# K pages turned on VectorE in 32x32 blocks, and scores in sixteen TensorE tiles

## The chip, the cores and the metric

The kernel runs on one core of a Trainium2 chip. The metric is device time in microseconds (us), from the start of the program to its end. A TensorE "pass" below is one matmul record of the profile with its weight load: a matmul on f32 operands leaves two such records, one on fp32r operands leaves one.

## The reference

One step of a small hybrid decoder: a gated short-convolution layer, then shared keys and values, then one attention layer with per-head forget values. The part that the change touches is the attention of the 64 new sample tokens (8 sequences of 8 tokens, 16 heads of 64) over 2048 past keys a sequence, which lie in 16 pages of 128 rows:

```python
s = jnp.einsum('nqhd,nkhd->nhqk', q, k).astype(jnp.float32) * (HEAD_DIM ** -0.5)
s = s + (jnp.transpose(fq, (0, 2, 1))[:, :, :, None] - jnp.transpose(fk, (0, 2, 1))[:, :, None, :])
p = jax.nn.softmax(jnp.where(mask[None, None], s, -jnp.inf), axis=-1)
return jnp.einsum('nhqk,nkhd->nqhd', p.astype(v.dtype), v)
```

`page_table` says which pages of `cache_k` and `cache_v` belong to a sequence. A page of K or of V is 128 rows of 1024 floats, 512 KB.

## The kernel before

After the convolution layer (to about 300 us) and the projection of all queries (to about 364 us), a loop of eight rounds does the rest; it is called `heads(i)` on every engine. Round i does two things at once: the past attention of sample sequence i over its 16 K pages and 16 V pages, and for the pair of heads 2i, 2i+1 the projection of K, V and the gate z, and the prompt's attention in four blocks. A last stage (from about 899 us) merges the new tokens and multiplies by the output weights.

**Pages.** SyncE loads them (`load_page`, L374 to L377) into a ring of 8 slots, 8 pages ahead, in the order K0 to K15, V0 to V15. A K page's slot is free when TensorE has turned it (wait on `b_t1`, L432), a V page's when its product is done (`b_used`, L434). In the same queue, in order, stand the round's other loads: `f_broad` at n=0, one weight block of 512 KB at n=0, 4 and 12, one `suffix` block of 256 KB at n=4, 8, 12 and 16, each behind waits of its own.

**Scores of a K page.** TensorE turns the page with 8 transposes of 128x128 (`turn`, L1201) into two PSUM banks; ScalarE copies one half out (L666) and VectorE the other (L1009). Two pages make a unit. `unit_scores` (L1393) multiplies the turned unit by the queries in 8 matmuls, each 128 rows by 32 columns of the array (four column tiles), 256 columns of data, f32. VectorE adds the forget term and takes the maximum (`add_suffix`, L1014). There are 8 units a round. Between the pages TensorE does single pieces of the K and V projections (`project` and `piece`, L1221; a piece is six matmuls; 8 pieces make one projection).

**After the last unit** TensorE turns the new K and V rows, and does the first prompt block's scores. VectorE makes the shift of the softmax, ScalarE takes exp of the scores (L707, four parts), and TensorE turns the four parts into `p_turned`. Then the 16 V pages follow (L1519), with the prompt's blocks between them. The sum of squares for the norm of the new K (L1426, L1427) stands among the K pages (k == 9), and ScalarE, then GpSimd (L514), finish that norm there.

**The end of a round.** VectorE multiplies the prompt's output by the gate (L1123), ScalarE copies it as fp32r (L766), and VectorE takes the difference (L1127).

All engines run their own instruction order as written; nothing but semaphores ties them.

Of the kernel before, what the change touches and what calls it, by code (L numbers as in the profile page):

```python
# [31 lines left out]
P = 128  # L32
# [20 lines left out]
STREAM = 2 * NPG  # L53
SLAB = 256
# [46 lines left out]
def build(nc, ctx, x_prompt, x_sample, state_conv, cache_k, cache_v, cache_logf, page_table,  # L101
# [33 lines left out]
    KTS = [place("k_turned", [P, KT, 2 * PAGE])]  # L135
    PTS = place("p_turned", [P, NPG, P])
    KTS.append(place("k_turned_odd", [P, KT, 2 * PAGE], over=at["p_turned"]))
# [36 lines left out]
    QC = place("q_current", [P, KT, 32])  # L174
# [7 lines left out]
    CS = place("logf_sums", [P, H, PAGE], over=at["sample_scores"])  # L182
    STN = place("state_rows", [2 * NB, D], over=at["suffix"])
# [5 lines left out]
    WHB = place("w_high_b", [P, KT, SLAB], F32R, over=at["k_turned"])  # L189
# [8 lines left out]
    QF = place("queries", [P, KT, TOK], over=at["gated_high"])  # L198
    FA = place("f_raw", [H, TOK], over=at["k_t"])
# [46 lines left out]
    b_used, b_qc, b_qt = sem("v_page_used"), sem("q_current_ready"), sem("q_pair_ready")  # L246
# [49 lines left out]
    def _(sp):  # L296
# [77 lines left out]
        def load_page(b, n):  # L374
            page = sp.value_load(PTAB[0:1, bass.ds(b * NPG + n % NPG, 1)], min_val=0, max_val=n_pool - 1)
            src = (kpages if n < NPG else vpages)[bass.ds(page, 1), :, :]
            sp.dma_start(ring[:, n % RING, :], src.rearrange("a p n -> (a p) n")).then_inc(b_page[n % RING], 16)  # L377
# [23 lines left out]
        def heads(i, last):  # L401
            for n in range(STREAM):
                if n == 0:
                    sp.wait_ge(b_c0f, 8 * i)
                    sp.wait_ge(b_c1f, 8 * i)
# [10 lines left out]
                if n in (4, 8, 12, 16):  # L416
                    c = n // 4 + 1
                    if not (last and c >= 4):
                        sp.wait_ge(b_c1f, 8 * i + n // 4)
                        load_suffix(i + c // 4, c % 4)  # L420
# [21 lines left out]
        sp.wait_ge(b_t1f, 24 * NB)  # L442
# [17 lines left out]
    def _(pool):  # L460
# [29 lines left out]
        for b in range(NB):  # L490
            pool.dma_start(suffix_dram[b].rearrange("h (g n) -> g h n", g=NPG),
                           CS[b * NPG:(b + 1) * NPG, :, :]).then_inc(s_sfx_st, 16)
# [10 lines left out]
        for n in range(10):  # L503
            scale_b(n % 2, n // 2 + 1, G_B if n < KT else G_KV)
        pool.wait_ge(q_out, KT)
        pool.tensor_copy(QC[:, :, :], QZ[:, 0, :, :]).then_inc(b_qc, 1)
        pool.tensor_copy(QT[:, :], QF[:, 0, 0:SEQ]).then_inc(b_qt, 1)

        def heads(i, last):
# [5 lines left out]
            if not last:  # L515
                scale_b(1, 7 + 2 * i, G_KV)
                pool.wait_ge(b_c1, 8 * i + 4)
                pool.tensor_copy(QC[:, :, :].rearrange("p k n -> p (k n)"),
                                 QZ[:, bass.ds(i + 1, 1), :, :].rearrange("p a k n -> p (a k n)")).then_inc(b_qc, 1)
                pool.wait_ge(b_c0, 8 * i + 8)  # L520
                pool.wait_ge(b_c1, 8 * i + 8)
# [8 lines left out]
    def _(act):  # L530
# [124 lines left out]

        act_done = ch.n


        def heads(i, last):
            t0 = [0]  # L660

            def turned0(out, src):

                act.wait_ge(b_t0, 24 * i + t0[0] + 1)
# [3 lines left out]
            for k in range(NPG):  # L668
                c = (k % 2) * PAGE
                if k % 2 == 0 and k >= 4:  # L670
                    act.wait_ge((b_c0, b_c1)[k // 2 % 2], 8 * i + k // 4)
                turned0(KTS[k // 2 % 2][:, 0:4, c:c + PAGE],
                        PS[:, T0, :].rearrange("p (k n) -> p k n", k=4)).then_inc(b_t0f, 1)
                if k == 6:
                    pr, sa = both(D0)
                    act.wait_ge(b_proj, KT + 3 * i + 1)
                    act.wait_ge(b_gl, i)
                    act.wait_ge(b_ddve, i + 1)
                    act.activation(prompt2(SQ[:, 0:SEQ]), pr, ACT.Square)
                    act.activation(SQ[:, SEQ:TOK], sa, ACT.Square).then_inc(b_dact, 1)  # L680
                if k == 10:
                    high_b(KT + 3 * i + 2, 1)
                if k == 14:
                    pr, sa = both(D0)
                    act.wait_ge(b_proj, KT + 3 * i + 2)
                    act.activation(prompt2(VT[:, 0:SEQ]), pr, ACT.Copy)
                    act.activation(VT[:, SEQ:TOK], sa, ACT.Copy).then_inc(b_dact, 1)
                if k == 9:

                    act.wait_ge(b_ss, i + 1)  # L690
                    act.wait_ge(b_normed, i)
                    act.activation(RR[:, SEQ:TOK], PS[:, OS, 0:NS], ACT.Ln, bias=EPSB(P), scale=1.0 / HD)
                    act.activation(RR[:, 0:SEQ], PS[:, OP, :], ACT.Ln, bias=EPSB(P), scale=1.0 / HD).then_inc(b_ln, 1)
                    act.wait_ge(b_ln, i + 1)
                    act.activation(RR[:, :], RR[:, :], ACT.Exp, scale=-0.5).then_inc(b_rr, 1)
            if not last:
                high_b(KT + 3 * i + 3, 0)

            act.wait_ge(b_kpo, 16 * i)
            act.wait_ge(b_vpo, 16 * i)  # L700
            turned0(KN[:, 0:QB, :], PS[:, T0, :].rearrange("p (k n) -> p k n", k=4)).then_inc(b_t0f, 1)
            turned0(VN[:, :, :], PS[:, T0, :].rearrange("p (k n) -> p k n", k=4)).then_inc(b_t0f, 1)
# [10 lines left out]
            act.wait_ge(b_t0f, 24 * i + 18)  # L713
            act.wait_ge(b_t1f, 24 * i + 17)
# [45 lines left out]
            assert t0[0] == 24  # L760
# [32 lines left out]
    def _(dve):  # L793
# [129 lines left out]
        def low_b(n, slot, to=None):  # L923
# [5 lines left out]
        dve.tensor_tensor(CS[:, :, :], PS[:, 7, 0:H].unsqueeze(2).to_broadcast([P, H, PAGE]), CS[:, :, :],  # L929
                          ALU.subtract).then_inc(s_sfx, 1)  # L930
# [38 lines left out]
        def query(m, s):  # L969
# [3 lines left out]
            dve.scalar_tensor_tensor(prompt2(QF[:, bass.ds(m, 1), 0:SEQ].rearrange("p a n -> p (a n)")), pr, GQ[:, 0:1],  # L973
                                     prompt2(RR[:, 0:SEQ]), ALU.mult, ALU.mult)
# [26 lines left out]
        def heads(i, last):  # L1001
# [3 lines left out]
            def turned1(out, src):  # L1005

                dve.wait_ge(b_t1, 24 * i + t1[0] + 1)
# [3 lines left out]
            def add_suffix(u):  # L1011

                free, bank = ((b_c0f, C0), (b_c1f, C1))[u % 2]
                dve.tensor_tensor_reduce(  # L1014
                    SS[:, u * 256:(u + 1) * 256], PS[:, bank, 0:256],
                    SFX[:, (u // 2) % 2, (u % 2) * 256:(u % 2) * 256 + 256],
                    1.0, NEG, ALU.add, ALU.max, TINY[:, 4 + u:5 + u]).then_inc(free, 1)

            for k in range(NPG):
                c = (k % 2) * PAGE  # L1020
                if k % 2 and k >= 3:
                    u = k // 2 - 1
                    if u % 2 == 0:
                        dve.wait_ge(b_sfx[(u // 2) % 2], (2 * i + u // 4 + 1) * 16)
# [613 lines left out]
```

## Time and profile before

| | us |
|---|---|
| median of 3 runs (lowest, highest) | 971.62 (970.4, 973.45) |
| the profiled execution | 975.04 |
| its span, first to last instruction | 973.2 |

In a row of a timeline the first number is the start in us from the start of the span, the second the duration in us, then come the engine, the line of the kernel, the operation, what it writes and reads, and how many instructions were merged. In brackets stands how long the engine had been idle before, and who ended that.

### The profile page before, as it was taken

The numbers are of one execution on the slowest core, as the hardware profiler recorded it, in microseconds if no ns is written. First come the engines' busy times: TensorE is split into PE (matmuls) and PEld (weight loads), VectorE is DVE, ScalarE is ACT, GpSimd is POOL, SyncE is SP. The second block draws the span as 40 slices with busy tenths as digits, with TensorE's granted clock in tenths as the row PEclk, the third lists the DMA queues.
The fourth block names the chain that finished last, engine by engine and source line by source line (L and its number), as shares of the span: only waits on it lengthen the run. The fifth ranks groups of instructions, "written<-read, shape, count | busy, mean of one in ns | idle before, by whom it ended". The sixth has DMA issues, their size and how long they took to land.

```text
span 973.2 us, 23705 instructions
## 1 busy us (share of the span) xinstructions
PE 939.5 (97%) x8516; PEld 802.0 (82%) x8516; DVE 486.6 (50%) x1133; ACT 385.1 (40%) x728; POOL 167.4 (17%) x111
## 2 busy tenths in 40 slices
PE   4999999999999999999999999999999999999998
PEld 4999999999998987868768778688687686776898
DVE  5675444556355334554544544645545545445632
ACT  5333333332144443543444534535434445345210
POOL 2233444332030311102002002011020020000000
PEclk9999999999999999999999999999999999999999
DMA  7233222225343527799799798798996997987412
GB/s 233 66 87 86 86 76 75 85 65 130 120 165 103 174 55 228 254 329 341 237 360 313 249 364 290 247 376 261 315 350 237 362 323 244 365 297 249 142 44 98
DMA packets 133334, 206.41 MB, mean 212 GB/s; under 512 B 8848, under 2 KB 91457, under 8 KB 133171
## 3 DMA queue, kind: packets, MB, share of 16 engines
q1 hardware_dynamic: 121602, 198.35, 60.7%
q10 hardware_dynamic: 11168, 5.51, 2.0%
q0 software_dynamic: 528, 2.10, 0.8%
q8 instruction: 21, 0.34, 0.2%
q14 instruction: 15, 0.11, 0.0%
HBM read 195.29 MB, written 10.63 MB: 212 GB/s over the span
## 4 chain that ended last, share of the span: by engine, by line
PE 82%; DMA 7%; ACT 4%; DVE 4%; issue 2%; SPq 1%; ACTq 0%; DVEq 0%
PE psum L1221 40%; PE psum L1201 16%; PE psum L1270 9%; PE psum L1404 7%; PE psum L1519 4%; DMA page_ring<-in_cache_k 4%; ACT sample_scores L707 2%; DMA w_raw<-in_a_w_out 2%; PE psum L1469 1%; PE psum L1447 1%; DMA residual<-in_x_prompt 1%; PE psum L1319 1%; PE psum L1427 1%; PE psum L1449 1%; DMA page_ring<-in_cache_v 1%
## 5 line engine op out<-in xcount | busy, mean ns | idle before, releaser
L1221 PE MATMUL psum<-xn_high,w_high 128*128 128x256 f32 (+1 forms) x992 | 237.2, 318 | 2.6 <-DVE w_low L832 2.6
L1221 PE MATMUL psum<-xn_low,w_high 128*128 128x256 f32 (+1 forms) x992 | 216.4, 297 | 0.0
L1221 PE MATMUL psum<-xn_high,w_low 128*128 128x256 f32 (+1 forms) x992 | 216.3, 297 | 0.0
L1221 PEld LDWEIGHTS psum<-xn_high,w_high 128*128 128x128 f32 x992 | 163.9, 191 | 20.2 <-issue 16.6
L1221 PEld LDWEIGHTS psum<-xn_high,w_low 128*128 128x128 f32 x992 | 169.0, 191 | 0.0
L1221 PEld LDWEIGHTS psum<-xn_low,w_high 128*128 128x128 f32 x992 | 168.9, 190 | 0.0
L1201 PE MATMUL psum<-constants,page_ring 128*128 128x128 f32 x1024 | 137.5, 277 | 7.7 <-DMA page_ring<-in_cache_k 6.5
L1201 PEld LDWEIGHTS psum<-constants,page_ring 128*128 128x128 f32 x1024 | 114.8, 141 | 35.1 <-issue 33.4
L501 POOL TENSOR_TENSOR w_raw<-w_raw,gains 128x1024 f32<-128x1024 f32 x32 | 60.8, 1899 | 338.9 <-DMA w_raw<-in_b_w_in 220.7
L1009 DVE COPY k_turned_odd<-psum 128x512 f32<-128x512 f32 x64 | 44.2, 691 | 93.5 <-PE psum L1201 93.5
L832 DVE TENSOR_TENSOR w_low<-w_raw,w_high 128x1024 fp32r<-128x1024 f32 x32 | 51.4, 1606 | 72.6 <-ACT w_high L565 72.6
L1009 DVE COPY k_turned<-psum 128x512 f32<-128x512 f32 x64 | 44.2, 690 | 71.5 <-PE psum L1201 71.3
L478 POOL TENSOR_TENSOR w_raw<-w_raw,gains 128x1024 f32<-128x1024 f32 x30 | 62.5, 2083 | 88.7 <-DMA w_raw<-in_a_w_in 88.7
L666 ACT ACTIVATE k_turned<-psum 128x512 f32<-128x512 f32 x64 | 38.2, 597 | 96.5 <-PE psum L1201 96.4
L1519 PE MATMUL psum<-page_ring,p_turned 128*32 128x256 f32 x1024 | 75.2, 388 | 0.9 <-DMA page_ring<-in_cache_v 0.8
L565 ACT ACTIVATE w_high<-w_raw 128x1024 fp32r<-128x1024 f32 x32 | 33.9, 1060 | 89.0 <-PE psum L1221 63.5
L666 ACT ACTIVATE k_turned_odd<-psum 128x512 f32<-128x512 f32 x64 | 38.1, 596 | 71.3 <-PE psum L1201 71.3
L1270 PE MATMUL psum<-w_high,gated_high 128*128 128x256 f32 (+1 forms) x160 | 46.5, 290 | 4.4 <-DVE w_low L859 1.9
L926 DVE TENSOR_TENSOR w_low<-w_raw,w_high 128x1024 fp32r<-128x1024 f32 x30 | 36.9, 1231 | 18.2 <-ACT w_high L615 18.2
L1270 PE MATMUL psum<-w_low,gated_high 128*128 128x256 f32 (+1 forms) x160 | 45.7, 286 | 0.0
L1270 PE MATMUL psum<-w_high,gated_low 128*128 128x256 f32 (+1 forms) x160 | 45.7, 286 | 0.0
L1270 PE MATMUL psum<-w_high_b,gated_high 128*128 128x256 f32 (+1 forms) x160 | 45.3, 283 | 0.1
(236 smaller groups left out, 1420.2 us busy)
## 6 DMA issues: line engine op xcount, KB each, us to landing
page_ring<-in_cache_k SPq DMA_DIRECT2D x128, 512.0 KB, 5.6
page_ring<-in_cache_v SPq DMA_DIRECT2D x128, 512.0 KB, 4.8
w_raw<-in_a_w_in SPq DMA_DIRECT2D x30, 512.0 KB, 4.1
suffix<-suffix_scratch SPq DMA_DIRECT2D x32, 256.0 KB, 4.8
w_raw<-in_b_w_in SPq DMA_DIRECT2D x16, 512.0 KB, 6.2
w_raw<-in_kv_w SPq DMA_DIRECT2D x16, 512.0 KB, 6.1
w_raw<-in_a_w_out SPq DMA_DIRECT2D x4, 1024.0 KB, 5.1
f_broad<-f_scratch SPq DMA_DIRECT2D x8, 512.0 KB, 6.2
```

The source lines that it names most:

```text
L478: pool.tensor_tensor(WR[:, q % 2, :, :], WR[:, q % 2, :, :], gain(G_A), ALU.mult).then_inc(a_scaled, 1)
L501: pool.tensor_tensor(WR[:, slot, :, :], WR[:, slot, :, :], gain(g), ALU.mult).then_inc(b_scaled, 1)
L565: act.activation(WH[:, slot, :, :], WR[:, slot, :, :], ACT.Copy).then_inc(a_high, 1)
L666: return act.activation(out, src, ACT.Copy)
L832: dve.tensor_tensor(WL[:, slot, :, :], WR[:, slot, :, :], WH[:, slot, :, :].bitcast(F32), ALU.subtract).then_inc(a_split, 1)
L926: dve.tensor_tensor(lo, WR[:, slot, :, :], h.bitcast(F32), ALU.subtract).then_inc(b_split, 1)
L1009: return dve.tensor_copy(out, src)
L1201: return pe.transpose(out, src, CT[0:r, C_ID:C_ID + r])
L1221: mm = pe.matmul(PS[:, bank + h, 0:c.stop - c.start], w[:, k, :], x[:, k, c], start=(k == 0 and n == 0), stop=(k == KT - 1 and n == 2))
L1270: mm = pe.matmul(PS[0:r, bank, 0:SLAB], x[:, k, toks(t)], wp[:, k, :], start=(k == 0 and p == 0), stop=(k == KT - 1 and p == 2))
L1404: mm = pe.matmul(PS[32 * j:32 * j + 32, bank, 0:256], QC[:, 2 * j + pp, :], KTS[u % 2][:, 2 * j + pp, :], start=(pp == 0), stop=(pp == 1), ...
L1519: mm = pe.matmul(PS[32 * j:32 * j + 32, OS, 0:4 * HD], PTS[:, k, 32 * j:32 * j + 32], ring[:, n % RING, 4 * HD * j:4 * HD * (j + 1)], star ...
```

## The change

1. VectorE turns each K page where it lies in the ring, with one `transpose` of 128x1024 that turns each block of 32x32 by itself. The transposes by TensorE and the copies of `k_turned` by ScalarE and VectorE are gone.
2. Four pages make a unit, so there are 4 units a round. `unit_scores` has 128 matmuls on 32 rows by 32 columns of the array (16 tiles), 128 columns of data each, f32; row tile r writes the bank C0+r, so the four banks C0, C1, OP, OS hold a unit's scores, and one matmul of a single column on bfloat16 stands ahead of them.
3. The queries lie in blocks for that (`q_blocks`), made once a round by GpSimd from `q_quarters`, which 16 matmuls make once, ahead of the loop.
4. TensorE's first part of a round is a loop of two, in each four pieces, a unit, four pieces, a unit; the pieces are the K projection's in the first and the V projection's in the second. The squares and the whole of the gate projection follow.
5. The ring's K slots come free four at a time, when a unit is scored. V pages are read in another order of rows, since the scores come out with their rows in that order; the `suffix` values are stored so too.
6. VectorE's order in a round: turns of pages 4 to 7, `add_suffix(0)`, copies of the K projection, turns 8 to 10, `add_suffix(1)`, turns 11 to 13, the low half of the gate's weights, turns 14 and 15, `add_suffix(2)` and `(3)`. Turns 0 and 1 of the next round stand ahead of the output's gating, 2 and 3 behind it.

```diff
@@ SyncE
                     if n < NPG:
-                        sp.wait_ge(b_t1, 24 * i + n + 1)
+                        if n % GROUP == 0:
+                            sp.wait_ge(b_su, NG * i + n // GROUP + 1)
                     else:
                         sp.wait_ge(b_used, NPG * i + n - NPG + 1)
@@ ScalarE, the order in a round
+            act.activation(prompt2(SQ[:, 0:SEQ]), pr, ACT.Square)
...
+            high_b(KT + 3 * i + 2, 1)
...
+            act.activation(prompt2(VT[:, 0:SEQ]), pr, ACT.Copy)
...
+            act.wait_ge(b_ss, i + 1)
...
+            act.activation(RR[:, 0:SEQ], PS[:, T1, :], ACT.Ln, bias=EPSB(P), scale=1.0 / HD).then_inc(b_ln, 1)
...
+            act.activation(RR[:, :], RR[:, :], ACT.Exp, scale=-0.5).then_inc(b_rr, 1)
...
+            turned0(VN[:, :, :], PS[:, T0, :].rearrange("p (k n) -> p k n", k=4)).then_inc(b_t0f, 1)
+            turned0(KN[:, 0:QB, :], PS[:, T0, :].rearrange("p (k n) -> p k n", k=4)).then_inc(b_t0f, 1)
             if not last:
                 high_b(KT + 3 * i + 3, 0)
...
             act.wait_ge(b_nbs, i + 1)
@@ VectorE
+        def turn_pages(i, ks):
+            for k in ks:
+                dve.wait_ge(b_page[k % RING], (4 * i + k // RING + 1) * 16)
+                dve.transpose(ring[:, k % RING, :], ring[:, k % RING, :]).then_inc(b_kt, 1)
@@
+            if not last:
+                turn_pages(i + 1, range(2))
             dve.wait_ge(b_po, i + 1)
             dve.wait_ge(b_sz, i + 1)
             dve.tensor_tensor(SQ[:, 0:SEQ], PS[:, OP, :], SZ[:, 0:SEQ], ALU.mult).then_inc(b_gf, 1)
...
             dve.tensor_tensor(gl, SQ[:, 0:SEQ], gh.bitcast(F32), ALU.subtract).then_inc(b_gl, 1)
+            if not last:
+                turn_pages(i + 1, range(2, GROUP))
@@ TensorE
+            def unit_scores(a, u):
+                pe.wait_ge(b_kt, NPG * i + 2 * GROUP * a + GROUP * (u + 1))
+                pe.wait_ge(b_suf, NG * i + 2 * a + u)
+                pe.matmul(PS[:, OS, 511:512], IDB[:, :], CMB[:, 0:1], start=True, stop=True)
+                for xf in range(8):
                     for j in range(4):
+                        c = 8 * j + xf
+                        for r in range(4):
+                            mm = pe.matmul(PS[32 * j:32 * j + 32, C0 + r, 0:P], QD[32 * r:32 * r + 32, c, :],
+                                           ring[32 * r:32 * r + 32, GROUP * u:GROUP * (u + 1), 32 * c:32 * c + 32],
+                                           start=(xf == 0), stop=(xf == 7), tile_position=(32 * r, 32 * j))
+                mm.then_inc(b_su, 1)
...
+            with pe.Fori(0, 2) as a:
+                pieces(a, range(0, 4))
+                pe.wait_ge(b_qd, i + 1)
...
+                pe.wait_ge(b_gf, i)
+                unit_scores(a, 0)
+                pieces(a, range(4, 8))
+                unit_scores(a, 1)
```

## Rows read from the trace of the kernel before

**Rows 1.** The page: TensorE's busy time, and GB/s of all DMA in 40 slices.
```profile
PE 939.5 (97%) x8516; PEld 802.0 (82%) x8516; DVE 486.6 (50%) x1133; ACT 385.1 (40%) x728; POOL 167.4 (17%) x111
GB/s 233 66 87 86 86 76 75 85 65 130 120 165 103 174 55 228 254 329 341 237 360 313 249 364 290 247 376 261 315 350 237 362 323 244 365 297 249 142 44 98
```
**Rows 2.** The chain of waits of the whole run, and one piece of it.
```profile
PE 82%; DMA 7%; ACT 4%; DVE 4%; issue 2%; SPq 1%; ACTq 0%; DVEq 0%
...
628.20 5.28 DMA page_ring<-in_cache_k
```
**Rows 3.** Engines by stretch: K pages of a round, then the rest of it.
```profile
633.60:670.50 36.90, 36.84 (x346) 30.90 (x347) 15.74 (x35) 14.61 (x26) 6.82 (x4) 1.00 1.01 347
671.50:700.30 28.80, 27.61 (x297) 18.19 (x293) 17.43 (x61) 15.64 (x40) 1.01 (x2) 1.00 0.79 258
```
**Rows 4.** TensorE's timeline among the K pages of a round.
```profile
638.59 1.03 PE L1201 MATMUL psum<-constants,page_ring 128*128 128x128 f32 x8
639.38 0.51 PE L1221 MATMUL psum<-xn_high,w_high 128*128 128x256 f32 x2
...
640.35 1.07 PE L1404 MATMUL psum<-k_turned,q_current 128*32 128x256 f32 x16
641.35 1.09 PE L1201 MATMUL psum<-constants,page_ring 128*128 128x128 f32 x8
```
**Rows 5.** Groups by line and shape, TensorE: all transposes of K pages.
```profile
L1201 PE MATMUL psum<-constants,page_ring 128*128 128x128 f32 x1024 | 137.5, 277 | 7.7 <-DMA page_ring<-in_cache_k 6.5 <-DVE k_turned L1009 1.2
```
**Rows 6.** TensorE's timeline: two row tiles side by side, and four column tiles.
```profile
608.18 0.92 PE L1447 MATMUL psum<-k_t,q_t 64*128 64x384 f32 x4
...
898.97 1.99 PE L1537 MATMUL psum<-ks_t,q_spread 128*32 128x64 f32 x128 [0.17 <-issue]
```
**Rows 7.** One line of VectorE: count, shortest, median and longest duration in ns.
```profile
L926 DVE TENSOR_TENSOR w_low<-w_raw,w_high x30: 1206/1219/1624, 311.4 to 861.2; 128x1024 fp32r<-128x1024 f32 x30
```
**Rows 8.** SyncE's timeline of DMA issues over the start of a round.
```profile
628.20 9.01 SPq L377 DMA_DIRECT2D page_ring<-in_cache_k  x8
637.92 0.40 SPq L407 DMA_DIRECT2D f_broad<-f_scratch  x1
...
639.94 4.16 SPq L377 DMA_DIRECT2D page_ring<-in_cache_k  x4
...
649.73 4.13 SPq L377 DMA_DIRECT2D page_ring<-in_cache_k  x4
```
**Rows 9.** DMA issues of 630 to 641, then of 633.6 to 646: count, KB, median us to landing.
```profile
page_ring<-in_cache_k SPq DMA_DIRECT2D x7, 512.0 KB, 5.8
...
page_ring<-in_cache_k SPq DMA_DIRECT2D x7, 512.0 KB, 7.3
```
**Rows 10.** Timelines of TensorE, VectorE and ScalarE where one round ends and the next begins.
```profile
633.60 1.09 PE L1201 MATMUL psum<-constants,page_ring 128*128 128x128 f32 x8 [0.70 <-DMA page_ring<-in_cache_k]
...
632.92 0.69 DVE L1123 TENSOR_TENSOR squares<-psum,silu_z 128x512 f32<-128x512 f32 x1
634.53 0.69 DVE L1127 TENSOR_TENSOR gated_low<-squares,gated_high 128x512 f32 x1 [0.93 <-ACT gated_high L766]
...
633.74 0.63 ACT L766 ACTIVATE gated_high<-squares 128x512 f32 x1 [0.29 <-DVE squares L1123]
```
**Rows 11.** Timelines behind the last unit of a round: ScalarE, TensorE, and GpSimd's norm.
```profile
608.68 0.71 ACT L707 ACTIVATE sample_scores<-sample_scores,tiny 128x512 f32<-128x512 f32 x1
...
604.30 1.07 PE L1404 MATMUL psum<-k_turned_odd,q_current 128*32 128x256 f32 x16
...
614.23 0.64 PE L1519 MATMUL psum<-page_ring,p_turned 128*32 128x256 f32 x8
...
657.93 1.43 POOL L514 TENSOR_TENSOR k_t<-k_t,rsqrt 128x576 f32<-128x576 f32 x1 [2.51 <-ACT rsqrt L695]
```
**Rows 12.** TensorE after an idle time, and the granted clock of the stretch that follows.
```profile
902.85 0.36 PE L1270 MATMUL psum<-w_high,gated_high 128*128 128x256 f32 x1 [1.88 <-DVE w_low L859]
...
904.00:908.00 4.00, 4.00 (x25) 4.00 (x24) 1.55 (x7) 2.41 (x15) 0.00 (x0) 0.62 0.88 287
```

More of the change, by code:

```diff
@@ L53 @@
 STREAM = 2 * NPG
+GROUP = 4
+NG = NPG // GROUP
 SLAB = 256
@@ L504, in _, with block_queries @@
             scale_b(n % 2, n // 2 + 1, G_B if n < KT else G_KV)
+        def block_queries(b):
+            own = QN[:, bass.ds(b, 1), 0:2 * H * NQ].rearrange("p a (j x f q) -> p x (a j) f q", x=4, f=2, q=NQ)
+            to = QD[:, :, :].rearrange("p (j x f) n -> p x j f n", x=4, f=2)
+            for x in range(4):
+                ins = pool.tensor_copy(to[:, x, :, :, NQ * x:NQ * x + NQ], own[:, x])
+            ins.then_inc(b_qd, 1)
+        pool.wait_ge(b_proj, 2)
+        pool.memset(QD[:, :, :], 0.0).then_inc(s_qz, 1)
         pool.wait_ge(q_out, KT)
-        pool.tensor_copy(QC[:, :, :], QZ[:, 0, :, :]).then_inc(b_qc, 1)
         pool.tensor_copy(QT[:, :], QF[:, 0, 0:SEQ]).then_inc(b_qt, 1)
+        pool.wait_ge(s_qne, 4)
+        pool.wait_ge(s_qz, 1)
+        block_queries(0)
         def heads(i, last):
@@ L662, in turned0 @@
             def turned0(out, src):
-                act.wait_ge(b_t0, 24 * i + t0[0] + 1)
+                act.wait_ge(b_t0, 8 * i + t0[0] + 1)
                 t0[0] += 1
                 return act.activation(out, src, ACT.Copy)
[L668 to L695, printed above, removed]
@@ new lines, in heads @@
+            turn_pages(i, range(4, 8))
+            add_suffix(0)
+            dve.wait_ge(b_proj, KT + 3 * i + 1)
+            pr, sa = both(D0)
+            gk = GAIN[:, G_K:G_K + 1]
+            dve.tensor_scalar(prompt2(KN_T[:, 0:SEQ]), pr, gk, None, ALU.mult)
+            dve.tensor_scalar(KN_T[:, SEQ:TOK], sa, gk, None, ALU.mult).then_inc(b_ddve, 1)
+            turn_pages(i, range(8, 11))
+            add_suffix(1)
+            turn_pages(i, range(11, 14))
+            low_b(KT + 3 * i + 2, 1)
@@ L1362, in _ @@
         pe.wait_ge(s_fnr, 1)
+        pe.wait_ge(q_out, KT)
+        pe.wait_ge(s_bf, 3)
+        for c in range(4):
+            for r in range(4):
+                mm = pe.matmul(PS[32 * r:32 * r + 32, T0 + c, :].rearrange("p (m n) -> p m n", m=KT),
+                               CT[:, C_ID + 32 * c:C_ID + 32 * c + 32], QF[:, :, SEQ:TOK],
+                               start=True, stop=True, tile_position=(0, 32 * r))
+        mm.then_inc(s_qn, 1)
         def heads(i):
@@ L1388, in project @@
                 for k in ks:
[L1389 removed]
+                    mm = piece(1, k, D0)
                 if ks[-1] == KT - 1:
                     mm.then_inc(b_proj, 1)
[L1393 to L1407 removed]
@@ new lines, in pieces @@
+            def pieces(a, ks):
+                with pe.If(a):
+                    if ks[0] == 0:
+                        pe.wait_ge(b_t0f, 8 * i)
+                        pe.wait_ge(b_t1f, 8 * i)
+                    for k in ks:
+                        mm = piece(0, k, T0)
+                    if ks[-1] == KT - 1:
+                        mm.then_inc(b_proj, 1)
+                with pe.Else():
+                    if ks[0] == 0:
+                        pe.wait_ge(b_split, KT + 3 * i + 2)
+                        pe.wait_ge(b_sz, i)
+                    for k in ks:
+                        mm = piece(1, k, D0)
+                    if ks[-1] == KT - 1:
+                        mm.then_inc(b_proj, 1)
@@ L1437, in block_scores @@
+            pe.matmul(PS[:, T1, :], CT[:, C_ONESB:C_ONESB + P], SQ[:, 0:SEQ], start=True, stop=True).then_inc(b_ss, 1)
             def block_scores(r):
```

246 lines of the change are left out of this document (110 added, 136 removed).

## The prediction, as it was made before the result was known

> **What bounds the kernel now.** I read the page first. TensorE is busy 97% of the span, twice as much as any other engine [rows 1], and 82% of the chain of waits is its work [rows 2]. That says: take work off TensorE. The second view speaks against it. In the eight rounds all DMA moves 240 to 376 GB/s, up from 66 to 90 in the first stage [rows 1], and by stretch the DMA engines are busy for 1.01 of the time among the K pages of a round, at 347 GB/s, and for 0.79 in the rest [rows 3]. The one DMA piece that recurs in the chain is K page 0 of the next round [rows 2]; TensorE waits 0.70 us for it [rows 10]. So TensorE sets the time, and right behind it stands the supply of pages. A round takes 700.3 - 633.6 = 66.7 us; I count its time from 633.0, where TensorE ended the round before, 0.7 ahead of 633.60.
>
> **When the pages come (kept by the change).** SyncE issues 8 K pages from 628.20 in 9.01 us [rows 8], one in (9.01 - 0.34) / 7 = 1.24 us. Page 0 lands 5.28 us after its issue [rows 2], at +0.5 us of the round; the others follow 1.24 to 1.28 apart, so page 3 at about +4.5 and page 7, issued at 636.9 and landing after 5.8 [rows 9], at +9.7. Behind them stand `f_broad` and a weight block. Pages 8 to 11 are issued from 639.94 over 4.16 us, the last at 643.8, and land after 7.3 us [rows 8, 9]: page 11 at +18.1. Pages 12 to 15 are issued to 653.5 and, by the 5.8 to 7.3 us of rows 9, land to about +27. In all that time the queue is full [rows 3], so an earlier issue brings none of them earlier.
>
> **Part 1, turning on VectorE.** TensorE loses 128 transposes a round: 8 in 0.79 us (638.59 to 639.38) [rows 4], 16 times: 12.6 us bare, and 137.5 / 8 = 17.2 us by the group [rows 5]. VectorE gets 16 turns of 128x1024 f32. No row shows one. From below: 1024 elements can't take less than the 0.69 us of a 512-element line [rows 10], in a faster mode, 0.7 us. From above: twice the two-input line on as many elements, 2.4 us. The nearest row is that line itself, 1.22 us [rows 7]; I take 1.25. It takes 20 us of VectorE, which sheds 16 copies of 0.69.
> The Trainium skill, "Vector Engine (DVE) Microarchitecture Reference", The reshape front-end and per-opcode configuration, says that a 32x32 transpose is pipelined to one element a cycle and lane. No row shows it; by it the turn would cost as the row on 1024 elements, and the sum stays.
>
> **Part 2, the scores.** Gone: 8 units of 16 passes, 1.00 us each (640.35 to 641.35) [rows 4]: 8.0 us a round. New: 4 units of 128 matmuls, 256 passes each. A pass of 256 columns on four column tiles costs 1.00 / 16 = 62 ns, with the switch of shape in it. One of 64 columns costs 1.77 us / 128 = 14 ns: its 128 passes are 1.99 us long [rows 6], less the last one's 0.22. Per column and tile that is 14 x 4 / 64 = 0.87 ns. Row tiles too run side by side: 4 passes of 384 columns on two row tiles take 0.92 us [rows 6], where one after the other they would be 4 x 384 x 0.87 = 1.34. 128 columns are then 111 ns a pass, by 16 tiles 7 ns: 256 x 7 = 1.8 us a unit at best. At 14 ns, the densest issue that a row shows, it is 3.6 us. At worst 16 tiles run as four: 111 / 4 = 28 ns, 7.1 us. I take 9 ns, between the first two, and 0.3 for the switch: 2.6 us.
> The trace has passes at 14 ns. The Trainium skill, "TensorE: Matmul & The Clock Gate", Wait — 56ns, not 53.3ns?, says that start-to-start never drops below about 25 ns; the trace disagrees for tiles. By that rule a unit would be 6.4 us, an estimate, and the whole the rival of slow tiles below.
>
> **Part 3, the round's start.** VectorE turns page 0 at +0.5 to 1.8, page 1 to 3.1. The gating (0.69), ScalarE's copy and VectorE's difference stand behind that now: 632.92 to 635.22 is 2.3 us [rows 10], so they end at 5.3. Pages 2 and 3 are turned by 7.8. TensorE has four pieces ahead of the first unit, 4 x 0.8 = 3.2 us (639.38 to 640.35 is one, 0.97 with the switch) [rows 4], and then waits 4.5 us. Unit 0: 7.8 to 10.4. Four pieces to 13.6. Pages 4 to 7 are turned by 12.8; unit 1: 13.6 to 16.2. Slots 0 to 3 come free at 10.4, so pages 8 to 11 are issued 11.2 to 14.9, 3 to 4 us later than before, and still land to +18.1 or little later. `add_suffix(1)` (512 elements, 0.7 us by rows 10) and page 11 end at 20; unit 2: 20 to 22.6, pieces to 25.8. Pages 12 to 15 are issued behind unit 1 and land to +27; page 15 is turned at 28.9 behind the weights' low half, 1.22 [rows 7]. Unit 3: 29.0 to 31.6. Before, the last unit ended 18.8 + 8.9 us ahead of the round's end [rows 11], at +39.0. So 7.4 us come in here, of the 12.6 + 8.0 - 4 x 2.6 = 10.2 that TensorE is given.
>
> **Part 4, behind the last unit.** Before, exp began 608.68 - 605.37 = 3.3 us after it, and the first V page 8.9 us after it (614.23) [rows 11]. Now the squares (1.1 us) stand there, then ScalarE's two Ln and Exp (1.7 us by the 0.7 of rows 11), and GpSimd's 1.43 us [rows 11] to +4.4; TensorE's three gate pieces (2.4), V turns and a fourth piece cover that to +4.9. Then come the K turns (0.5), ScalarE's copy (0.6) and its high half of weights, moved behind that copy (some 1.1 us for twice the elements of its copy). Exp begins at +7.3, 4.0 later than before, and the rest follows as before: first V page at +12.9. The V pages keep their 633.0 - 614.23 = 18.8 us.
> A round: 31.6 + 12.9 + 18.8 = 63.3 us against 66.7: 3.4 less, eight times 27 us.
>
> **Part 5, once.** 16 matmuls of 512 columns ahead of the loop are 32 passes on four column tiles, twice the columns of a 62 ns pass: 4.0 us. The copies behind them stand beside the first four pieces. The sum: -27 + 4 = -23 us. Against its own 975.04 us that is 952; against the median, 3.4 us lower, 949. I predict 950.
>
> **Costs set at nothing.** The copies taken from ScalarE were hidden: it is busy 40% [rows 1]. GpSimd's `block_queries` waits for the last unit of a round and has 30 us until the next first one. The V pages' new order of rows keeps 4 KB a row; a costlier issue would delay V0 to V7, which have about 5 us to spare. SyncE waits for a unit with `suffix` and weight blocks queued behind; their users come later than before.
>
> **The rivals.**
> *Dear turns (slower).* A turn of 2.1 us makes VectorE the chain of the first part: from +0.5, 16 turns and 6.5 us of its other lines put unit 3 at +40.6 instead of 29.0, the round at 74.9, the whole at 952 + 8 x 11.6 = 1045. It decides from 1.6 us on, where the round is 66.7. For it: nothing shows the instruction. Against: 1.22 us for as many elements with two inputs.
> *Slow tiles (slower).* With 7.1 us a unit TensorE's own order binds: 7.8 + 4 x 7.1 + 9.6 = 45.8, the round 77.5, the whole 952 + 8 x 14.2 = 1066. It decides from 4.4 us a unit. For it: the two passes of a matmul go to one tile, and the second must wait for the first. Against: four tiles keep this pace already.
> *The change of bound costs the gain (within 15 us of before).* TensorE now idles 4.5 us at each start. After 1.88 us idle the granted clock was 0.62 over 904 to 908, that is 1.2 GHz for three of those 4 us [rows 12]. One such fall a round where TensorE binds costs half of the three, 1.5 us, and a page later by one service time 1.3: 65 to 66.5 a round, 962 to 977. For it: both are in the rows.
> *TensorE alone sets the time (faster).* Then a round loses 12.6 + 8.0 and gains 4 x 2.6: 56.5 us, 897 in all. Against: 1.01 DMA share among the K pages [rows 3]. Half of it, should pages come earlier than I have them: 925 to 937.
>
> **How the numbers follow.** My forecast, 938 to 962: 0.50. TensorE alone or half of it: 0.12. The gain lost: 0.17. Dear turns 0.09, slow tiles 0.12. The likeliest gives 950. The range of 922 to 1000 takes in the first, the third, half of the second and the slow rivals' mild forms (a turn of 1.75 us, a unit of 5 us give about 1000): 0.79. A measurement tells 0.3% from no change, 2.9 us: faster 0.71 (the first two and half of the third), same 0.05, slower 0.24.
>
> **What would show it.** Turns near 1.25 us on VectorE; units of 2 to 3.6 us on TensorE; an idle time of 4 to 5 us ahead of each round's first unit, ended by a VectorE turn, and one ahead of the fourth; DMA share near 1 in the first 27 us of a round; first V page 12 to 13 us after the last unit; rounds of 63 us. Units over 4.4 us, turns over 1.6 us or rounds under 60 us make it wrong.

## The result: 1047.03 us, 7.9% slower, and its profile

The changed kernel takes 1047.03 us (1045.41 to 1050.35, 4 runs) against 971.01 (970.16 to 973.45, 4 runs): ratio 1.0787, interval 1.0757 to 1.0817. The forecast was 950 us. Ratios compare the fast executions of each kernel; where only one execution is fast, the table calls the ratio unclear. From the profile's page of the changed kernel (busy time; queue of instruction packets: packets, MB, share; costliest groups):

```profile
PE 915.1 (87%) x14724; PEld 795.0 (76%) x14724; DVE 570.3 (54%) x1111; ACT 311.3 (30%) x602; POOL 176.2 (17%) x136
...
q8 instruction: 86, 1.41, 0.5%
...
PE 65%; issue 11%; DMA 11%; DVE 4%; SPq 4%; ACT 4%; ACTq 0%; DVEq 0%
...
L1014 DVE STREAM_TRANSPOSE page_ring<-page_ring 128x1024 f32<-128x1024 f32 x128 | 154.0, 1229 | 51.1 <-DMA page_ring<-in_cache_k 50.5
...
L1433 PE MATMUL psum<-page_ring,q_blocks 32*32 32x128 f32 x8192 | 124.5, 291 | 26.8 <-issue 26.8
```

TensorE was relieved, from 97% to 87% [rows 1], and the time rose all the same. What took the room is named in the chain, where "issue" has 11% after 2% before [rows 2]: time in which TensorE waited for nothing that the profile shows. Its waits (total, times, longest, in us):

```profile
PE psum L1251 <- issue: 46.8, 15, 6.8
PE psum L1433 <- issue: 26.8, 16, 2.4
PE psum L1428 <- DVE tiny L1052: 13.3, 8, 3.0
```

73.6 us of TensorE's idle time have no releaser. One round in TensorE's timeline (start, duration, idle time before in brackets), from the last V page of a round to the last unit of the next and its end:

```profile
671.20 0.64 PE L1551 MATMUL psum<-page_ring,p_turned 128*32 128x256 f32 x8 [0.68 <-DMA page_ring<-in_cache_v]
678.63 0.82 PE L1251 MATMUL psum<-xn_high,w_high 128*128 128x256 f32 x2 [6.80 <-issue]
...
684.69 2.69 PE L1433 MATMUL psum<-page_ring,q_blocks 32*32 32x128 f32 x187
688.66 1.16 PE L1433 MATMUL psum<-page_ring,q_blocks 32*32 32x128 f32 x69 [1.28 <-issue]
...
693.17 1.99 PE L1433 MATMUL psum<-page_ring,q_blocks 32*32 32x128 f32 x136
697.24 2.22 PE L1433 MATMUL psum<-page_ring,q_blocks 32*32 32x128 f32 x120 [2.07 <-issue]
...
703.96 3.57 PE L1433 MATMUL psum<-page_ring,q_blocks 32*32 32x128 f32 x256
...
711.91 3.57 PE L1433 MATMUL psum<-page_ring,q_blocks 32*32 32x128 f32 x256
...
728.01 0.64 PE L1551 MATMUL psum<-page_ring,p_turned 128*32 128x256 f32 x8
...
747.02 0.64 PE L1551 MATMUL psum<-page_ring,p_turned 128*32 128x256 f32 x8 [0.25 <-DMA page_ring<-in_cache_v]
```

A round runs from 671.84 to 747.66: 75.8 us, against 66.7 before [rows 3] and 63.3 forecast. TensorE stands still for 6.80 us at its start though the profile shows nothing that the pieces there wait for, and stops in the middle of units 0 and 1. Units 2 and 3, the inner loop's second pass, run through. Unit 0 starts at +12.9. Unit 3 ends at +43.6, forecast 31.6; the first V page follows 12.5 us behind it and the V pages take 19.7. So all of the loss lies ahead of unit 3's end. The windows of the same round (the last three columns are granted clock, DMA share, GB/s):

```profile
671.90:682.00 10.10, 3.37 (x14) 3.40 (x15) 8.49 (x9) 1.01 (x2) 0.00 (x0) 0.63 1.03 404
682.00:695.00 13.00, 11.72 (x430) 10.60 (x428) 4.96 (x8) 0.76 (x3) 1.90 (x1) 0.90 0.35 108
```

Over the idle start and the pieces behind it the granted clock is 0.63 on average, that is 1.2 GHz for about three quarters of these 10.1 us. Unit 0 frees its slots late, and the DMA engines, which were full ahead of it, fall to 0.35.

### The profile page after: what moved, and what is told of

It is laid out like the page before. It is cut to its first block, busy times and chain, and to the rows that moved or that the text cites. A ratio compares the mean times of both kernels' runs of the same rounds, so it can differ in the third digit from the quotient of the medians.

```text
span 1048.5 us, 35591 instructions
## 1 busy us (share of the span) xinstructions
PE 915.1 (87%) x14724; PEld 795.0 (76%) x14724; DVE 570.3 (54%) x1111; ACT 311.3 (30%) x602; POOL 176.2 (17%) x136
## 4 chain that ended last, share of the span: by engine, by line
PE 65%; issue 11%; DMA 11%; DVE 4%; SPq 4%; ACT 4%; ACTq 0%; DVEq 0%
PE psum L1251 36%; PE psum L1433 9%; PE psum L1300 9%; DMA page_ring<-in_cache_v 5%; PE psum L1231 3%; PE psum L1551 3%; DMA suffix<-suffix_scratch 2%; SPq L379 2%; DMA page_ring<-in_cache_k 2%; ACT sample_scores L724 2%; SPq L384 2%; DMA w_raw<-in_a_w_out 1%; PE psum L1482 1%; PE psum L1504 1%; DMA residual<-in_x_prompt 1%
## 5 line engine op out<-in xcount | busy, mean ns | idle before, releaser
L1251 PEld LDWEIGHTS psum<-xn_high,w_high 128*128 128x128 f32 x992 | 175.7, 201 | 74.2 <-issue 70.2
L1251 PE MATMUL psum<-xn_low,w_high 128*128 128x256 f32 (+1 forms) x992 | 224.5, 307 | 0.0
L1014 DVE STREAM_TRANSPOSE page_ring<-page_ring 128x1024 f32<-128x1024 f32 x128 | 154.0, 1229 | 51.1 <-DMA page_ring<-in_cache_k 50.5
L1251 PEld LDWEIGHTS psum<-xn_low,w_high 128*128 128x128 f32 x992 | 178.0, 200 | 0.0
L1251 PEld LDWEIGHTS psum<-xn_high,w_low 128*128 128x128 f32 x992 | 176.8, 199 | 0.0
L1433 PE MATMUL psum<-page_ring,q_blocks 32*32 32x128 f32 x8192 | 124.5, 291 | 26.8 <-issue 26.8
L1433 PEld LDWEIGHTS psum<-page_ring,q_blocks 32*32 32x32 f32 x8192 | 103.9, 105 | 37.7 <-issue 31.1
L1052 DVE CUSTOM_DVE_ANT_1 sample_scores<-psum,suffix 128x512 f32<-128x512 f32 x32 | 34.4, 1076 | 29.5 <-issue 29.5
L938 DVE TENSOR_TENSOR residual<-psum,residual 128x256 f32<-128x256 f32 (+1 forms) x40 | 16.6, 420 | 55.1 <-PE psum L1300 54.9
L1551 PEld LDWEIGHTS psum<-page_ring,p_turned 128*32 128x32 f32 x1024 | 23.0, 108 | 29.5 <-issue 13.4
```

The lines of the kernel that those rows point to most:

```text
L1014: dve.transpose(ring[:, k % RING, :], ring[:, k % RING, :]).then_inc(b_kt, 1)
L1052: dve.tensor_tensor_reduce(out, PS[:, C0:OS + 1, 0:P], later, 1.0, NEG, ALU.add, ALU.max, TINY[:, 4 + u:5 + u]).then_inc(b_suf, 1)
L1251: mm = pe.matmul(PS[:, bank + h, 0:c.stop - c.start], w[:, k, :], x[:, k, c], start=(k == 0 and n == 0), stop=(k == KT - 1 and n == 2))
L1433: mm = pe.matmul(PS[32 * j:32 * j + 32, C0 + r, 0:P], QD[32 * r:32 * r + 32, c, :], ring[32 * r:32 * r + 32, GROUP * u:GROUP * (u + 1), 32 ...
L1551: mm = pe.matmul(PS[32 * j:32 * j + 32, OS, 0:4 * HD], PTS[:, k, 32 * j:32 * j + 32], ring[:, n % RING, 4 * HD * j:4 * HD * (j + 1)], star ...
```

## The experiments

Two theories are put to the test, S and U. Theory S: the 6.80 us are TensorE waiting for its instructions. The page has 86 instruction packets, the kernel before 21; the rounds' body grew from 1,390 to 1,877 instructions (counted in the compiled program), and in the 450 us from 450 to 900 the trace of the kernel before has none of that queue. Theory U: the time lies in the work (units, suffix additions, the gating).

The trace also says when each of these packets is under way (0.9 to 1.5 us each in after's rounds), and that ties them to the stops. In the round shown, one packet runs from 675.46 to 676.43, and TensorE goes on at 678.63; one from 686.22 to 687.18, and it goes on at 688.66; one from 694.82 to 695.87, and it goes on at 697.24. In the rounds of after there are 23 stops put down to issue that are longer than 0.8 us. All of them end behind the end of a packet, by 1.3 to 1.5 us inside the units and by 2.2 to 2.4 us at a round's start. In a_flat it is 1.2 to 1.6 us for all 28 such stops, in b_pad_flat 1.3 to 1.8 us for all 20. Chance would not do that: in after the packets come 8 us apart on average.

| kernel | what differs | us | ratio to before (95%) |
|---|---|---|---|
| b_two | before, body of two rounds | 1001.65 | 1.0344 (1.0295 to 1.0393) |
| b_flat | before, rounds written out | 976.05 | 1.0059 (1.0038 to 1.0080) |
| b_pad_loop | before, 256 more passes a round, looped | 1019.08 | 1.0488 (1.0459 to 1.0518) |
| b_pad_flat | the same, written out | 1098.91 | 1.1328 (1.1268 to 1.1388) |
| a_flat | after, all loops written out | 1128.92 | 1.1661 (1.1616 to 1.1705) |
| a_inner | after, inner loop written out | 1136.58 | 1.1729 (1.1696 to 1.1761) |
| a_outer | after, outer loop written out | 1064.50 | 1.0953 (1.0892 to 1.1013) |
| a_onepath | after, If and Else merged | 1046.92 (1017.55 to 1057.12) | unclear |
| a_wide | after, units of half the instructions | 996.25 | 1.0300 (1.0240 to 1.0360) |
| a_wide84 | a_wide, wider matmuls | 1003.10 | 1.0326 (1.0286 to 1.0365) |
| a_wide_light | a_wide, half of the K bytes | 960.53 | 0.9896 (0.9852 to 0.9940) |
| a_wide_turns | a_wide, two turns earlier | 978.29 | 1.0064 (1.0039 to 1.0089) |
| b_coarse | before, K slots reloaded by fours | 973.04 | 1.0036 (1.0015 to 1.0057) |
| a_light | after, half of the K bytes | 1007.65 | 1.0369 (1.0316 to 1.0422) |

**Does the length of the program alone cost time? b_two, b_flat, b_pad_loop, b_pad_flat.** No part of the change is in these four.

```
 b_two:   for i2 in Fori(0, NB // 2):  heads(2 * i2); heads(2 * i2 + 1)
 b_flat:  for i in range(NB):  heads(i)
 b_pad_loop, ahead of unit 7:
+    with pe.Fori(0, 8) as q:
+        for n in range(4):          # b_pad_flat: for n in range(32), no Fori
+            for j in range(4):
+                pe.matmul(PS[32*j:32*j+32, OS, 508:509], CT[:, 32*j:32*j+32], CT[:, 0:1], ...)
```

> The kernel before with one edit: TensorE's loop runs four times over two rounds instead of eight times over one, so its body is some 2,780 instructions instead of 1,390; the work and every wait are the same. Theory S: the body no longer fits, each of the four jumps costs 5 to 8 us, 20 to 35 us more than before (990 to 1010 us), and the trace has instruction packets in the rounds, where before has none. Theory U: within 3 us of before.

> The kernel before with TensorE's eight rounds written out straight, no jump at all. Theory S in its narrow form (only the jump back costs, straight code is fetched ahead in time): within 5 us of before, with some 45 instruction blocks fetched over the rounds. Theory S in its wide form (any fetch costs, whichever way it is reached): 15 us or more slower. Theory U: within 3 us of before.

> The kernel before with 128 more matmuls a round on TensorE (32x32 tiles, one column, into a PSUM column that nobody reads), 512 instructions, written as a loop of 8 times 64 instructions: the rounds' body has 1,459 instructions. At the 14 ns a pass of before's tiles they take 3.6 us a round, 29 us in all. Theory S (instruction supply, store somewhere between 1,390 and 1,880 instructions): the body still fits, some 1,000 us, no instruction packets in the rounds. Theory U: some 1,000 us.

> The same 128 matmuls a round in the same place, written out: the body has 1,902 instructions, as many as after's 1,877, and TensorE executes the same matmuls as in the looped twin. Theory S: the body is fetched anew in each round, 30 to 60 us above the twin (1,030 to 1,060 us), with 7 to 9 instruction blocks a round in the trace and an idle time of 5 to 7 us put down to issue at each round's start. Theory U: the twin's time within 3 us.

The instruction packets on the pages of b_two, b_flat, b_pad_loop and b_pad_flat, one line each:

```profile
q8 instruction: 66, 1.08, 0.4%
```
```profile
q8 instruction: 58, 0.95, 0.4%
```
```profile
q8 instruction: 21, 0.34, 0.1%
```
```profile
q8 instruction: 93, 1.52, 0.6%
```

b_two does the work of before and takes 32 us more, as theory S expected. The padded pair executes the same matmuls and differs by 79.8 us: its bodies have 1,459 and 1,902 instructions, and only the longer one brings packets into the rounds. TensorE's longest stops in b_pad_flat, in the added matmuls and at the round's start behind them:

```profile
655.98 1.63 PE L1476 MATMUL psum<-constants 128*32 128x1 f32 x174
660.83 1.33 PE L1476 MATMUL psum<-constants 128*32 128x1 f32 x82 [3.22 <-issue]
...
698.80 1.96 PE L1201 MATMUL psum<-constants,page_ring 128*128 128x128 f32 x8 [5.66 <-issue]
```

That is the picture of the changed kernel in one that has nothing of the change. Theory U is refuted for these; theory S's sizes were too low (the pair was expected 30 to 60 us apart, and the looped one at 1,000 us; of the looped one's 48 us its added passes take 8 x 4.00 = 32, the rest was not taken apart). b_flat shows the other side: written out, each round's 1,390 instructions are fetched too (58 packets), but TensorE has no stop of any weight put down to issue, and it costs 6 us in all. That this is so because they are used up slowly, 1,390 in 66.7 us, fits, but no run varies it alone.

**Is it the jump or the rate? a_flat, a_inner, a_outer, a_onepath.**

```
 a_inner:  for a in range(2): ... if a: ... else: ...   (in place of pe.Fori, pe.If, pe.Else)
 a_flat:   a_inner, and for i in range(NB): heads(i)
 a_outer:  after, and for i in range(NB): heads(i)
 a_onepath, pieces(a, ks): no If; PS[:, bass.ds(2 * a + h, 1), ...], WH[:, 0, k, :] in both passes
```

> The kernel after with TensorE's program written out straight: its eight rounds one behind the other and the two halves of the K part as Python code, so that no branch is taken in the rounds; waits, matmuls and the other engines are the same. Theory S (instruction supply: the rounds' loop body of TensorE no longer stays in its instruction store and each jump back costs TensorE some 6.8 us idle with nothing to wait for, and smaller gaps follow): the idle time put down to issue goes, unit 0 starts at +8 us of the round as predicted, rounds of 64 to 67 us, 950 to 980 us in all. Theory U (the time lies in the work itself: units of 3.57 us, strided suffix additions, the gating ahead of the turns): 1040 to 1050 us, unchanged.

> The kernel after with only TensorE's inner loop of two passes and its If and Else written out; the loop over the eight rounds stays, its body grows from some 1,900 to some 2,900 instructions. Theory S: one jump back a round is left, with its 6.8 us, and the gaps inside the K part that came from the inner jump and the If go: 1000 to 1030 us, more instruction packets than after's 86 since more than the body's blocks are fetched in each round. Theory U: 1040 to 1050 us.

> The kernel after with TensorE's loop over the eight rounds written out straight and the inner loop of two passes kept, with its If and Else: the work is that of after, 1,877 instructions a round stand in the program, and the second inner pass runs again through instructions just used. Theory J (most of the loss is the jump back to instructions that are gone, 6.8 us idle at each round's start): unit 0 starts at +8 to +9 of the round, 990 to 1,010 us. Theory F (a block of 256 instructions takes some 4 to 5 us to come, and units that use one in 1.8 us outrun it, jump or no jump): the idle time moves from the round's start into units 0 and 1, 1,035 to 1,055 us.

> The kernel after with the If and Else of the inner loop merged into one path, which takes its PSUM banks from the loop's variable and the weights of K in both passes (so v is K's projection without its own weights); matmuls and columns are as many as in after. The rounds' body shrinks from 1,877 to 1,793 instructions, seven blocks of 256 (an instruction packet carries 16 KB). Theory S with a store of eight such blocks and all of them usable: no packets in the rounds, 960 to 990 us. Theory S with one or two blocks given to reading ahead: 1,030 to 1,047 us. Theory U: 1,040 to 1,050 us.

I had expected straight code to cure it, and missed a_flat by 150 us and a_inner by 107 us. Without any jump unit 0 does start at +8 (633.08, where the round began at 625.1), but then TensorE stops inside the units. TensorE's waits and unit 1 of a_flat:

```profile
PE psum L1433 <- issue: 87.1, 33, 5.2
```
```profile
642.17 2.90 PE L1433 MATMUL psum<-page_ring,q_blocks 32*32 32x128 f32 x205
648.65 1.42 PE L1433 MATMUL psum<-page_ring,q_blocks 32*32 32x128 f32 x51 [3.58 <-issue]
```

a_outer says the same with the inner loop kept: unit 0 starts at +9.2 (690.13, where the round began at 680.9) after no stop at the start, only a wait of 5.71 us for a turn, and the stops have moved into the units:

```profile
690.13 3.50 PE L1433 MATMUL psum<-page_ring,q_blocks 32*32 32x128 f32 x164
694.98 1.45 PE L1433 MATMUL psum<-page_ring,q_blocks 32*32 32x128 f32 x92 [1.35 <-issue]
...
700.40 1.77 PE L1433 MATMUL psum<-page_ring,q_blocks 32*32 32x128 f32 x113
703.45 1.89 PE L1433 MATMUL psum<-page_ring,q_blocks 32*32 32x128 f32 x128 [1.28 <-issue]
709.92 0.68 PE L1433 MATMUL psum<-page_ring,q_blocks 32*32 32x128 f32 x15 [4.58 <-issue]
...
715.80 3.57 PE L1433 MATMUL psum<-page_ring,q_blocks 32*32 32x128 f32 x256
```

Unit 2, which runs again through instructions just used, is whole. That is theory F, though at 1064.50 us the kernel is slower than its 1,035 to 1,055. So the rate decides, not the jump alone: 256 passes are 512 instructions in 3.57 us, and the supply doesn't keep up. A packet carries some 258 of them (a_flat's program of 27,350 came in 106 packets). The jump adds its stop at the start, but a body that is fetched whole loses more without the inner loop (1128.92 and 1136.58 us) than with it (1047.03). The body of 1,793 instructions of a_onepath still isn't kept: 68 packets, 42 of them between 450 and 890 us. Its times scatter, so nothing is read from them. For these kernels the border lies between 1,459 and 1,793; where exactly, no run says.

The Trainium skill ("Runtime: NRT & Kernel Launch", Instruction fetch mechanics) describes a refill in blocks of 16 KB, as the packets show, and says that a long kernel is streamed, the cost of crossing into the next block being "mostly hidden". b_flat agrees, nearly; a_flat's 87.1 us don't. It also says that "there's no instruction cache that benefits from spatial locality"; here the loops of before and b_pad_loop run from 450 to 890 us without a packet.

**What is the change worth with its instructions at hand? a_wide, a_wide84.**

```
-for xf in range(8):
+for xf in range(0, 8, 2):
     ...  mm = pe.matmul(PS[.., C0 + r, 0:2 * P], QD[..], ring[.., 4 pages, 32 * c:32 * c + 64], ...)
 a_wide84: 0:336 and 32 * c:32 * c + 84, c at most 29
```

> The kernel after with each unit's 128 matmuls of 128 columns turned into 64 of 256 columns: as many columns through the same 16 tiles by half the instructions (its output is not the scores any more, half of the feature blocks is taken with the wrong queries); the rounds' body shrinks from 1,877 to 1,363 instructions. Theory S: it fits, no instruction packets in the rounds, no idle time put down to issue at a round's start, units of 1.8 to 3.6 us, rounds of 62 to 66 us, 940 to 980 us in all: the prediction's own schedule. Theory U: the idle times stay, and the time falls by the shorter units at most: 1,000 to 1,050 us.

> The kernel with the wide units, their matmuls 336 columns wide instead of 256, so that a unit takes about as long as after's warm one (3.57 us instead of 2.7) by the same few instructions: what after would take if its instructions were always there. If units are on the path: 8 times 4 times 0.8, some 20 to 26 us more than the wide kernel, 1,015 to 1,022 us. If the supply of pages binds (theory P), one unit in two is covered: 1,000 to 1,012 us.

a_wide has 21 packets, as before, and no stop at a round's start. It missed its forecast of 940 to 980 us all the same. TensorE's two largest waits in it, and its timeline over one round from 713.08:

```profile
PE psum L1428 <- DVE page_ring L1014: 43.4, 15, 4.6
PE psum L1428 <- DVE tiny L1052: 17.3, 8, 3.4
```

```profile
712.44 0.64 PE L1551 MATMUL psum<-page_ring,p_turned 128*32 128x256 f32 x8 [0.29 <-DMA page_ring<-in_cache_v]
...
720.93 0.17 PE L1428 MATMUL psum<-causal_b,ident_b 128*128 128x1 bf16 x1 [3.94 <-DVE page_ring L1014]
721.04 4.05 PE L1433 MATMUL psum<-page_ring,q_blocks 32*32 32x256 f32 x128
...
728.43 2.76 PE L1433 MATMUL psum<-page_ring,q_blocks 32*32 32x256 f32 x128
...
737.16 0.17 PE L1428 MATMUL psum<-causal_b,ident_b 128*128 128x1 bf16 x1 [2.37 <-DVE page_ring L1014]
...
746.28 2.76 PE L1433 MATMUL psum<-page_ring,q_blocks 32*32 32x256 f32 x128
...
761.61 0.64 PE L1551 MATMUL psum<-page_ring,p_turned 128*32 128x256 f32 x8
...
779.88 0.64 PE L1551 MATMUL psum<-page_ring,p_turned 128*32 128x256 f32 x8 [0.30 <-DMA page_ring<-in_cache_v]
```

Unit 0 waits 3.94 us for a turn and starts at +8.0: the forecast's 4.5 and 7.8. Its unit is 2.76 us, the forecast's 2.6. Yet unit 2 starts at +24.2 instead of 20, and the round is 67.4 us instead of 63.3. Wider matmuls (3.29 us a unit) add 6.9 us to the whole; the two intervals in the table overlap, so this is a rough figure. So of the 76 us that after loses against before, up to 43.9 go with its instructions (1047.03 - 1003.10), and even then the change doesn't win. A few of the 43.9 may belong to the units, since a_wide84's are 3.29 us and not the 3.57 of after.

The 73.6 us of stops in after cost less than their sum, because TensorE would have stood waiting in part of them anyway: with its instructions at hand it waits 43.4 + 17.3 = 60.7 us for VectorE's turns and suffix additions, where after has 13.3 (`L1428 <- DVE tiny L1052`, the wait for a suffix addition). At a round's start the stop of 6.80 us makes unit 0 4.9 us later (+12.9 against +8.0).

**What holds the pages? a_wide_light, b_coarse, a_wide_turns.**

```
 a_wide_light: sp.dma_start(ring[:, n % RING, 0:512], src[:, 0:512])            for K pages
 b_coarse:     if n % 4 == 0: sp.wait_ge(b_t1, 24 * i + n + 4)                  in place of one wait a page
 a_wide_turns: turn_pages(i + 1, range(2, GROUP)) ahead of dve.wait_ge(b_gh, i + 1), not behind gated_low
```

> The kernel with the wide units (half the instructions, no fetches in the rounds, 996 us) with one more edit: of each K page only the first half of the columns is loaded (the first eight pages of all are loaded whole), so its scores are not those of the reference. Theory P (what is left above the forecast of 950 lies in the supply of pages: slots come free four at a time, and pages 8 to 15 land too late): units 2 and 3 start at about +20 and +29 of the round instead of +24.4 and +33.4, rounds of 62 to 64 us, 945 to 965 us. Theory O (it lies in TensorE's and VectorE's own order: the gating, the cold clock in unit 0, the copies behind K's projection): units 2 and 3 stay within 1 us of where they are, 985 to 1,000 us.

> The kernel before with one part of the change alone: SyncE reloads the ring's slots in the K part four at a time, when the fourth page is turned, instead of one by one. Theory P: in before four pages are turned in 9 us, so page 8 is asked for some 7 us later, TensorE waits for K pages in each round, 2 to 5 us a round, 985 to 1,010 us. Theory O: the ring's other four pages cover it, within 5 us of before.

> The kernel with the wide units, in which VectorE turns pages 2 and 3 of the next round ahead of the difference that makes gated_low instead of behind it. Theory R (the round waits for slots that are released late): unit 0 starts at +6 to +7 of the round instead of +8, pages 8 to 11 are asked for 1 to 2 us earlier, and rounds lose as much, 8 to 16 us in all: 980 to 989 us. Theory B (the bytes as such bind, or the later gated_low holds something up): 993 to 1,000 us.

In a_wide, SyncE's issues (start, duration, count) and the windows around them:

```profile
708.44 9.12 SPq L384 DMA_DIRECT2D page_ring<-in_cache_k  x8
...
726.05 3.91 SPq L384 DMA_DIRECT2D page_ring<-in_cache_k  x4
```
```profile
713.10:725.00 11.90, 7.50 (x153) 5.89 (x153) 10.28 (x10) 1.01 (x2) 0.00 (x0) 0.86 1.01 378
725.00:731.00 6.00, 6.00 (x164) 5.13 (x153) 3.50 (x7) 1.50 (x3) 1.90 (x1) 1.00 0.54 174
```

The queue, full until 725, runs half empty for 6 us, because unit 0 must end (at 725.09) before four slots are free at once. VectorE then stands waiting for single pages:

```profile
731.69 1.25 DVE L1014 STREAM_TRANSPOSE page_ring<-page_ring 128x1024 f32<-128x1024 f32 x1 [1.07 <-DMA page_ring<-in_cache_k]
733.61 1.25 DVE L1014 STREAM_TRANSPOSE page_ring<-page_ring 128x1024 f32<-128x1024 f32 x1 [0.68 <-DMA page_ring<-in_cache_k]
```

With half of the K bytes the same program takes 960.53 us, 35.7 less. The units of one of its rounds, from 629.1:

```profile
636.20 4.53 PE L1436 MATMUL psum<-page_ring,q_blocks 32*32 32x256 f32 x128
...
644.76 2.76 PE L1436 MATMUL psum<-page_ring,q_blocks 32*32 32x256 f32 x128
...
651.64 2.76 PE L1436 MATMUL psum<-page_ring,q_blocks 32*32 32x256 f32 x128
...
659.40 2.76 PE L1436 MATMUL psum<-page_ring,q_blocks 32*32 32x256 f32 x128
```

They start at +7.1, 15.7, 22.5 and 30.3. And two turns put ahead of one subtraction, with all bytes, are worth 18.0 us: in a_wide_turns unit 0 starts at 646.21, +6.3 of a round that began at 639.9. Releasing slots by fours is not bad in itself: in before it costs 2.6 us. By these two runs together it becomes bad where the ring's first half is held for 12 us; a kernel with wide units that releases slots one by one, which would show it directly, was not run.

**Do instructions come late because of the pages? a_light.** The edit of a_wide_light, in after.

> The kernel after (128 matmuls a unit, body too long) with only the first half of the columns of each K page loaded, as in the light wide kernel; its scores are not those of the reference. Theory Q (blocks of instructions come late because they queue behind pages): the idle time put down to issue falls from 74 us on TensorE to under 45, and the time by 40 us or more, below 1,005 us. Theory L (a block's delay does not depend on the pages' traffic): the idle time stays at 65 to 75 us, and the time falls only by what the pages' supply held up beside it, 1,025 to 1,047 us.

```profile
PE psum L1254 <- issue: 35.3, 15, 4.8
PE psum L1436 <- issue: 21.4, 16, 1.5
```

56.7 us instead of 73.6, with the longest stop 4.8 instead of 6.8, while K's traffic is halved: between the two theories. The time fell by 39 us, about what the same edit gave a_wide. The stops are shorter with less traffic, which speaks for some queueing behind pages; the packets themselves take no less (1.0 us each in both). How much of a block's way is fixed stays open.

## Why the prediction was wrong, by its steps

- *Part 1, the turn.* 1.25 us forecast, 1.229 measured. Right; the rival of dear turns fell with it. No row of before could show it.
- *Part 2, the unit.* 2.6 us forecast inside 1.8 to 3.6; a warm one is 3.57, 13.9 ns a pass, no faster than four tiles [rows 6]. The bound at which all 16 tiles run side by side (7 ns a pass) was the wrong one to lean to. Price: some 7 us by a_wide84, for half of the excess.
- *Part 3, "TensorE has four pieces ahead of the first unit".* This step failed. The sum had no term for the supply of instructions: it counted 256 passes a unit, but not that these are 512 instructions, and that two units written out carry the rounds' body from 1,390 to 1,877. "Costs set at nothing" should have named it, since the page lists instruction packets in a queue of their own. Price: up to 44 us, by the kernels with the wide units; that 443 instructions more in a body can do as much is shown by the padded pair. The rivals had none of this kind; "slow tiles" named the size (1066), but not the cause.
- *Part 3, "still land to +18.1 or little later".* It failed too, where instructions are at hand: page 10 is turned from 733.61, +20.5, and TensorE waits 2.37 us for the last turn of its four. The row that warned was read and not used: by [rows 3] the DMA engines are busy for 36.90 x 1.01 + 28.80 x 0.79 = 60.0 us of a round. A round of 63.3 leaves 3.3 us for holes, and one stretch of 6 us at 0.54 takes 2.8 of them. The same sum speaks against the rival of TensorE alone, at 56.5: three kernels with whole pages all have 60 to 61 us of DMA time in a round (66.7 x 0.92 before, 75.8 x 0.81 after, 67.4 x 0.89 in a_wide), though the rate at full share varies from 324 to 404 GB/s, so it is no hard floor. Halving K's bytes gives 36 us (a_wide_light); the order at the start alone gives 18 (a_wide_turns).
- *Part 3, "Unit 3: 29.0 to 31.6".* The sum lets unit 3 start as page 15 is turned, at 28.9. By the change's own text it also waits for `add_suffix(2)`, which VectorE does behind that turn: the wait `b_suf` of `unit_scores`. This term was left out, and an addition on 512 elements takes 1.08 us, not 0.7. In a_wide the turns end at 745.13, the addition at 746.11, and unit 3 starts at 746.28. It is at most some 1.1 us a round, 9 us in all, an estimate from these rows.
- *The clock.* Put at nothing but in a rival, "The change of bound costs the gain", it shows in the round of a_wide: unit 0 takes 4.05 us behind 3.94 us idle, and 2.76 where TensorE was busy; 1.3 us late, for the release of slots as well. That rival had the mechanism of what is left in a_wide, a cold clock and later pages, but too small, at 962 to 977 us for 996.
- *Part 4 and the V pages.* 12.9 and 18.8 us forecast; in a_wide 761.61 - 749.04 = 12.6 and 18.9. Right.
- *The balance.* 950 forecast. 960.5 is measured with light K pages; 36 more with whole ones; 7 more with longer units; 44 more with the instructions fetched: 1047. Each is the difference of one kernel and the next in this order, so they add up by construction; in another order the shares could be others.

No version of the change with all bytes beat the kernel before. The nearest, a_wide_turns, is at 1.0064 and takes units that can't be written so for real scores.

## What to carry to other kernels

Count the instructions of a loop's body before making work finer, and look for instruction packets inside the loop: on TensorE a body of 1,459 stayed and one of 1,793 didn't, and here it was dense small matmuls that outran the supply. Check each new wait of the changed code against the order of the engine that it waits for. Add up each resource's busy time over the loop, and treat what is left to the new time as the room for all holes together. Where slots are freed in groups, what delays the first group empties the queue.

## What the hardware showed beyond that

- Unrolling is no cure: after with everything written out is 82 us slower than after, while before written out is 0.6% slower than before.
- Passes on 32x32 tiles in 4 by 4 took 13.9 ns at 128 columns, 21.6 at 256 (2.76 us / 128) and 25.7 at 336 (3.29 / 128): by these three, some 45% of the cost at 128 columns does not go with the columns. One-column passes on four tiles took 9.4 ns written out (1.63 us / 174) and 15.6 in a loop of 32 passes:

```profile
693.17 4.00 PE L1477 MATMUL psum<-constants 128*32 128x1 f32 x256
```
